# The last block's input projection by 2x2 blocks with seven products, its token-major part and the linear recurrence inside it

## The chip, the cores and the metric

The kernel runs on one core of a Trainium2 chip. A core has TensorE (matmuls), VectorE, ScalarE, GpSimd and SyncE, each with an instruction queue of its own; they meet only at semaphores. The metric is the device time of one execution in microseconds (us). SBUF is the core's on-chip memory of 128 partitions, PSUM the memory into which TensorE accumulates.

## What is computed

Two models in a row on one sequence of 2048 tokens of width 1024: two blocks of a diffusion-style mixer, then one block of linear recurrences. All is fp32. The change is in the input projection of the last block and in two of its users:

```
def second_block(x, c, norm_w, w_ada, b_ada, w_in, ...):
    h = rmsnorm(x, norm_w) * (1 + scale) + shift
    p = h @ w_in                      # 2048 x 1024 by 1024 x N_IN
    # a_x 512, a_g 512, hg_q 512, hg_f 512, hg_i 512, hg_g 512, z 1024, xbc 1536, dt 16
    a = causal_conv(a_x, 4 taps); xbc = silu(causal_conv(xbc, 4 taps))
    y_lru = rg_lru(a, ...) * silu(a_g)
    # hg_f gives a log decay and its running sums; hg_i is wanted token-major
def rg_lru(x, wa, ba, wx, bx, lam):
    r = sigmoid(x @ wa + ba); i = sigmoid(x @ wx + bx)      # blocks of 64 x 64
    log_a = -8 * r * softplus(-lam); a = exp(log_a)
    b = sqrt(-expm1(2 * log_a)) * (i * x)
    h_t = a_t * h_(t-1) + b_t
```

## The kernel before

The program is a row of stages, each a block of five instruction lists (one per engine) with its own semaphores and an all-engine barrier at its end (`Stage`, L83). `program` (L2765) calls them. In the last block: `project` ("in_2", tensors `in_...` in the trace), `tokens_lru` ("hi_2", `hi_...`), `mixers` (`mix_...`), `project_out` (`out_...`).

**Matmuls in three parts.** An fp32 operand is split into a head (rounded to fp32r by ScalarE's copy) and a rest (operand minus head, by GpSimd or VectorE). A product is head x head + rest x head + head x rest (`PARTS`, L288), three matmuls in place of one. `h` holds heads and rests of the 1024 x 2048 columns, 8 tiles of 128 rows, for the whole of both stages.

**`project`** (L291). There are 41 tiles of 128 outputs: 4 `conv`, 12 `conv_silu`, 4 `decay`, 20 with Silu, 1 copy. Each takes 4 chunks of 512 columns x 3 parts x 8 rows of tiles = 96 matmuls (L450; the first two tiles at L436). TensorE runs tile behind tile; two PSUM halves of 2048 columns alternate, as do two weight buffers. ScalarE makes a tile's head (L463), GpSimd its rest (L615), and each tile is emptied by ScalarE (L505, L513, L489). For convolution tiles VectorE does 4 instructions of 2048 columns (L546, L549); for decay tiles ScalarE does Sigmoid, Abs, Exp, Ln and VectorE four steps that read PSUM (L556 to L564), and only then is the PSUM half free. GpSimd issues the stores.

**`tokens_lru`** (L1835). Of `w_hi` 512 columns, in 16 tiles of 128 tokens x 24 matmuls (L1909), with the recurrence in eight units of 128 channels x 1024 tokens between: gates on TensorE (L1898), Sigmoid, Tanh, Exp, Square, Sqrt on ScalarE (L1942 to L1955), products and the scan on VectorE (L1997 to L2009). It reads back `ax` and `gates`, which `project` stored.

The order is written by hand in each engine's list; no scheduler stands behind it. In the rows below `SPq` and `POOLq` are DMA issues on SyncE's and GpSimd's queues.

## Time and profile before

| | us |
|---|---|
| median of 3 runs (4538.61 to 4540.83) | 4540.7 |
| the profiled execution's own time | 4536.25 |
| its span in the profile | 4534.6 |
| TensorE busy | 3932.5 (87%) |
| VectorE, ScalarE, GpSimd busy | 2488.9, 1576.4, 1070.6 |
| `project` "in_2", first load to last matmul | 2550.9 to 3477.9 |
| seam to `tokens_lru`, until its matmuls run on | 3477.9 to 3518.1 |
| `tokens_lru` to its last matmul; to the mixers' first load | 3630.1; 3642.9 |

The profile is one execution. Its views used here: busy time by stretch (each engine's busy us and instruction count, the granted clock of TensorE as a share of 2.4 GHz, the DMA engines' busy share and GB/s), the chain of work that ended last, the timeline of an engine, and the durations of one line. Ends of matmuls are modelled and they are pipelined: a 128x512 matmul shows about 0.39 us though one ends every 0.23; a few records are missing, so durations of groups are used, not counts.

### The profile page before, as it was taken

To read this page: it belongs to the slowest core of one execution; us is meant where nothing else is said; L and a number is where in the kernel's file an instruction comes from. 1 tells how busy PE (TensorE), PEld (TensorE's weight loads), DVE (VectorE), ACT (ScalarE), POOL (GpSimd) and SP (SyncE) were. 2 spreads that over 40 slices of the span, in tenths; PEclk is the share of its full clock that TensorE was granted. 3 is DMA by queue.
4 is the path that set the end of the run, shared out by engine and by line. 5 is a ranking of instruction groups with operands and counts; after the bars stand their busy time and mean duration, and the time that the engine had idled before them with its cause. 6 is when DMAs were issued, how large, how long until landed. Compare 5 with 4: busy or idle time off the path is not lost. (4 is left out here: it accounts for less than half of the span.)

```text
span 4534.6 us, 51807 instructions
## 1 busy us (share of the span) xinstructions
PE 3932.5 (87%) x19448; PEld 3243.2 (72%) x19448; DVE 2488.9 (55%) x3379; ACT 1576.4 (35%) x2589; POOL 1070.6 (24%) x879
## 2 busy tenths in 40 slices
PE   4659998798796999879889799999997968886998
PEld 2548886687575888768657588878885757775886
DVE  2645943687375594378736643330000479995564
ACT  3331102676222110267522212231111755554331
POOL 1421110121111111012111111111110046664454
PEclk7779999899997999989999899999998989998999
DMA  6341122422474112232245421131111356554453
GB/s 236 106 164 56 70 79 88 100 64 83 142 248 142 59 70 79 89 100 66 83 154 205 170 84 70 70 144 70 77 75 65 127 153 151 148 140 162 177 193 114
DMA packets 315762, 529.50 MB, mean 117 GB/s; under 512 B 26790, under 2 KB 203686, under 8 KB 299592
## 3 DMA queue, kind: packets, MB, share of 16 engines
q1 hardware_dynamic: 277002, 353.97, 25.0%
q0 software_dynamic: 38544, 172.69, 10.2%
q8 instruction: 131, 2.15, 0.2%
q14 instruction: 85, 0.70, 0.1%
HBM read 373.57 MB, written 153.00 MB: 116 GB/s over the span
## 5 line engine op out<-in xcount | busy, mean ns | idle before, releaser
L450 PE MATMUL in_ps<-h,in_wp 128*128 128x512 f32 x6624 | 1508.4, 390 | 10.0 <-POOL in_wp L615 10.0
L450 PEld LDWEIGHTS in_ps<-h,in_wp 128*128 128x128 f32 x6624 | 1247.2, 188 | 270.9 <-POOL in_wp L615 11.6
L1714 PE MATMUL out_ps<-out_y,out_wp 128*128 128x512 f32 x2976 | 689.2, 393 | 33.1 <-ACT out_y L1569 25.9
L1714 PEld LDWEIGHTS out_ps<-out_y,out_wp 128*128 128x128 f32 x2976 | 562.0, 189 | 159.7 <-issue 31.8
L585 DVE SCALAR_TENSOR_TENSOR cy<-cu,in_cw,cy 128x2048 f32<-128x2048 f32 x120 | 314.5, 2621 | 4.3
L898 PE MATMUL att_O<-att_pT,att_vs 128*128 128x512 f32 x960 | 302.1, 423 | 0.0
L513 ACT ACTIVATE in_ob<-in_ps 128x2048 f32<-128x2048 f32 x37 | 69.7, 1884 | 664.0 <-PE in_ps L450 664.0
L1631 POOL TENSOR_TENSOR out_wp<-out_w,out_wp 128x2048 fp32r<-128x2048 f32 (+1 forms) x48 | 192.5, 4010 | 412.6 <-ACT out_wp L1562 412.4
L615 POOL TENSOR_TENSOR in_wp<-in_w,in_wp 128x1024 fp32r<-128x1024 f32 x75 | 201.4, 2687 | 284.4 <-ACT in_wp L463 249.7
L1022 DVE TENSOR_TENSOR att_pT<-att_T,att_pT 128x512 fp32r<-128x512 f32 x320 | 219.5, 686 | 73.4 <-ACT att_pT L951 65.1
L1977 DVE TENSOR_SCALAR hi_z<-hi_z 128x4 f32<-128x4 f32 x1 | 0.2, 172 | 463.6 <-ACT hi_z L1934 463.6
L1001 DVE CUSTOM_DVE_ANT_0 att_S<-att_S,att_mk,att_nsink 128x640 f32<-128x640 f32 x256 | 227.0, 887 | 8.0 <-PE att_S L878 7.7
L951 ACT ACTIVATE att_pT<-att_T 128x512 fp32r<-128x512 f32 x320 | 190.3, 595 | 89.0 <-PE att_T L886 88.8
L940 ACT ACTIVATE att_prob<-att_S,att_nm 128x640 f32<-128x640 f32 x256 | 203.7, 796 | 49.6 <-DVE att_nm L1001 44.7
L463 ACT ACTIVATE in_wp<-in_w 128x1024 fp32r<-128x1024 f32 x75 | 79.3, 1057 | 371.2 <-ACTq L481 226.1
L436 PE MATMUL in_ps<-h,in_wp 128*128 128x512 f32 x576 | 144.0, 414 | 63.9 <-ACT h L470 63.9
L886 PE MATMUL att_T<-att_ident,att_prob 128*128 128x128 f32 x1280 | 193.4, 274 | 0.0
L436 PEld LDWEIGHTS in_ps<-h,in_wp 128*128 128x128 f32 x576 | 113.4, 198 | 94.5 <-ACT in_wp L463 65.1
L832 POOL TENSOR_TENSOR att_qs<-att_qf,att_qs 64x512 fp32r<-64x512 f32 x64 | 82.2, 1285 | 384.6 <-ACT att_qs L933 384.6
L629 POOL DMA_DIRECT2D gates<-in_ob x36 | 20.6, 573 | 630.2 <-ACTq L516 630.2
L898 PEld LDWEIGHTS att_O<-att_pT,att_vs 128*128 128x128 f32 x960 | 157.2, 190 | 14.9 <-DVE att_pT L1022 0.9
L886 PEld LDWEIGHTS att_T<-att_ident,att_prob 128*128 128x128 f32 x1280 | 152.3, 141 | 10.9 <-DVE att_pT L1022 0.4
(485 smaller groups left out, 6209.3 us busy)
## 6 DMA issues: line engine op xcount, KB each, us to landing
in_w<-in_w_in SPq DMA_DIRECT2D x75, 512.0 KB, 3.3
gates<-in_ob POOLq DMA_DIRECT2D x36, 1024.0 KB, 4.2
out_w<-in_w_out SPq DMA_DIRECT2D x32, 1024.0 KB, 4.8
out_mw<-in_w_ada_rows SPq DMA_DIRECT2D x48, 512.0 KB, 3.6
att_qf<-q SPq DMA_DIRECT2D x64, 256.0 KB, 4.3
out_yr<-y SPq DMA_DIRECT2D x16, 1024.0 KB, 7.0
x<-out_x POOLq DMA_DIRECT2D x64, 256.0 KB, 3.8
out_yr<-y SPq DMA_DIRECT2D x32, 512.0 KB, 5.6
```

What stands on the lines that cost most here:

```text
L436: mm = nc.tensor.matmul(ps[:, q, cc], wp[:, q, i, k], h[:, j, k, cc], start=(n + k == 0), stop=(n == 2 and k == KT - 1))
L450: mm = nc.tensor.matmul(ps[:, q, c * W:(c + 1) * W], wp[:, q, i, k], h[:, j, k, c * W:(c + 1) * W], start=(n + k == 0), stop=(n == 2 and k ...
L585: stt(y[:, t], u[:, t, k:k + N], cw31[:, t, k:k + 1], y[:, t], ALU.mult, ALU.add).then_inc(tapped, 1)
L615: pool.tensor_tensor(wp[:, q, 1], wt[:, q], wp[:, q, 0].bitcast(F32), ALU.subtract).then_inc(parted, 1)
L886: tr = nc.tensor.transpose(psT[:, n % 2, j * P:(j + 1) * P], prob[:, b % 2, 2 * j + g, kt * P:(kt + 1) * P], ident[:])
L898: mm = nc.tensor.matmul(psO[:, b % 2], vs[:, at, part, g * HD:g * HD + P], pT[:, r, side], start=(u + n == 0), stop=(u == U - 1 and n == 2))
L940: nc.scalar.activation(prob[:, b % 2, hh], psS[:, n % 2, S0:S0 + NK], ACT.Exp, bias=nm[:, b % 2, hh:hh + 1], scale=-1.0, accum_out=den[:, ...
L951: nc.scalar.activation(pT[:, m % 4, 0], psT[:, n % 2], ACT.Copy).then_inc(led, 1)
L1001: nc.vector.tensor_tensor_reduce(out=S, in0=S, in1=m, scale=1.0, scalar=nsink[:, 1, hh:hh + 1], op0=ALU.add, op1=ALU.min, accum_out=nm[:, ...
L1022: tt(pT[:, m % 4, 1], psT[:, n % 2], pT[:, m % 4, 0].bitcast(F32), ALU.subtract).then_inc(freed, 1)
L1631: pool.tensor_tensor(wp[:, u % NW, 1], wt[:, u % 2], wp[:, u % NW, 0].bitcast(F32), ALU.subtract).then_inc(parted, 1)
L1714: mm = nc.tensor.matmul(ps[:, u % NB, :W], wp[:, u % NW, a, k], y[:, c % 2, b, k], start=(i + k == 0), stop=(i == 2 and k == KY - 1))
```

## The change

`project` and `tokens_lru` are replaced for the last block by one stage, `project_lru`. Its names:

- The sequence is worked in two halves of 1024 columns (p = 0, 1), each of V = 23 units: 22 pairs of output tiles (2 conv, 6 conv_silu, then decay, silu, decay, silu, eight silu, two hi) and one single tile (dt), between.
- A pair is a 2x2 block product: two tiles of outputs x two 512-row halves of the depth, by two chunks of 512 columns. It is done as seven products of 12 matmuls (3 parts x 4) in place of eight. `sums(i)` on VectorE makes the four combined weight blocks; `difference` on GpSimd makes the combined column blocks once per half; `h` holds seven column blocks.
- The products land in three PSUM banks (X, Y, Z) of a double buffer. ScalarE copies product 0 to `p1` (`first_product`) and empties X (`empty`); VectorE adds (`second`, `fourth` twice, `upper`, `lower`), each reading one PSUM bank.
- Each product has its own head (ScalarE) and rest (GpSimd), in a ring `wp` of four, three ahead.
- hi tiles come out channel-major and are turned on TensorE by 128x128 transposes (`turn`), copied by `move`, stored token-major.
- The recurrence's units run inside units 12 to 20 of each half, one per two units: gates on TensorE, the rest between the heads and additions. `decay` and the recurrence share buffers.
- SyncE issues all loads and stores; tiles leave through a ring `ob` of three slots. The weight layout is changed on the host in order only.

```diff
+    RING, AHEAD, NOB = 4, 3, 3
+    BANK = (X, Y, Z, Y, X, Y, Z)
+            def weights(i):
+                wait(sp, parted, base(i - 1) if i >= 2 else 0)
...
+                sp.dma_start(raw[:, i % 2, 0:n], w_d[t:t + n].rearrange("a p k n -> p a k n")).then_inc(w_in[i % 2], 16)
...
+                if i + 2 < NU:
+                    weights(i + 2)
+                if i >= 1:
+                    store(i - 1)
...
+            def difference(p, n):
+                for k in range(KH):
+                    if n == 2:
+                        pool.wait_ge(shifted, p * KT + KH + k + 1)
+                        tt(column(2, k), column(5, k), column(2, k), ALU.subtract).then_inc(differed, 1)
+                    elif n == 1:
+                        pool.wait_ge(hparted, p * 28 + k + 1)
+                        pool.wait_ge(differed, p * 16 + k + 1)
+                        tt(column(1, k), column(2, k), column(0, k), ALU.add).then_inc(differed, 1)
...
+            def product(i, n):
+                g = base(i) + n
+                if n == 0:
+                    wait(pe, emptied, i - 1)
+                elif n == 1 and i >= 2:
+                    pe.wait_ge(combined, combos(i - 1))
+                elif n == 3:
+                    pe.wait_ge(combined, combos(i) + 1)
+                elif n == 4:
+                    pe.wait_ge(copied, i + 1)
+                elif n >= 5:
+                    pe.wait_ge(combined, combos(i) + n - 3)
+                times(i, n, n, BANK[n], n < 3, g).then_inc(prod, 1)
...
+            def silus(i):
+                act.wait_ge(combined, combos(i + 1))
+                empty(i, ACT.Silu)
...
+            def fourth(i):
+                dve.wait_ge(prod, base(i) + 4)
+                tt(u4[:], p1[:], ps[:, i % 2, Y], add).then_inc(combined, 1)
+                dve.wait_ge(combined, combos(i) + 2)
+                if kind(i) in ("silu", "hi"):
+                    free(dve, i, 1)
+                tt(target(i, 1, 1), u4[:], ps[:, i % 2, Z], add).then_inc(combined, 1)
...
+            for i in range(NU + 1):
...
+                if i and pair(i - 1):
+                    lower(i - 1)
...
+                if convs:
+                    convolve(i - 1, 0)
...
+                if kind(i - 2) == "decay":
+                    decay(i - 2, 1)
...
+                second(i)
+                if convs:
+                    convolve(i - 1, 1)
+                if lru_of(i, 1) is not None:
+                    widen(lru_of(i, 1))
...
+                fourth(i)
+                if i + 1 < NU:
+                    sums(i + 1)
+                if kind(i - 1) == "decay":
+                    decay(i - 1, 0)
+                if lru_of(i, 1) is not None:
+                    double(lru_of(i, 1))
...
+                upper(i)
...
+                if lru_of(i, 1) is not None:
+                    scan(lru_of(i, 1))
...
-        with nc.sbuf_tensor("h_2", [P, 2, KT, SEQ], F32R) as h:
-            project(nc, "in_2", h, SEQ, t["w_in_2"], [("conv", 4, ax, 1.0), ("conv_silu", 12, xbc, 1.0), ("decay", 4, (hk, hcum, hkc), 1.0),
-                                                      (ACT.Silu, 20, gates, 1.0), (ACT.Copy, 1, dt, 1.0)],
-                    (xT, row12, gain2[:, :, 0], mod2[:, 0:KT, 0]), taps4=(t["taps_2"], t["tap_bias_2"]))
-            tokens_lru(nc, "hi_2", h, SEQ, t["w_hi_2"], HW, hi, ax, t["lru_wa_2"], t["lru_ba_2"], t["lru_wx_2"], t["lru_bx_2"],
-                       t["lru_lambda_2"], gates[0:4], y[0:4])
+        project_lru(nc, "in_2", t["w_in_2"], (xT, row12, gain2[:, :, 0], mod2[:, 0:KT, 0]), (t["taps_2"], t["tap_bias_2"]),
+                    (ax, xbc, hk, hcum, hkc, gates, dt, hi),
+                    (t["lru_wa_2"], t["lru_ba_2"], t["lru_wx_2"], t["lru_bx_2"], t["lru_lambda_2"], y))
```

How it stands in the built program, at three places. VectorE in the convolution tiles, before (after the columns are made):

```order
L528 SCALAR_TENSOR_TENSOR in_ob<-in_ob,gain,in_reset 128x512 x8
L531 SCALAR_TENSOR_TENSOR h<-in_ob,mod,h 128x512 x8
L534 MEMSET in_ub 128x2x3
L546 TENSOR_SCALAR in_ob<-in_ub,in_cw,in_cb 128x2048
L549 SCALAR_TENSOR_TENSOR in_ob<-in_ub,in_cw,in_ob 128x2048 x3
```

VectorE in a convolution unit now, from `second` to `lower` (L2413 `second`, L2449 to L2454 `convolve`, L2417 and L2421 `fourth`, L2403 to L2408 `sums`, L2428 `upper`, L2432 `lower`):

```order
L2413 TENSOR_TENSOR in_u<-in_p,in_ps 128x512
L2449 TENSOR_SCALAR in_ob<-in_ov,in_cw,in_cb 128x1024
L2452 SCALAR_TENSOR_TENSOR in_ob<-in_ov,in_cw,in_ob 128x1024 x3
L2454 COPY in_tails<-in_ov 128x3
L2417 TENSOR_TENSOR in_u<-in_p,in_ps 128x512
L2421 TENSOR_TENSOR in_ov<-in_u,in_ps 128x512
L2403 TENSOR_TENSOR in_S<-in_w 128x512
L2405 TENSOR_TENSOR in_S<-in_S,in_w 128x512
L2406 TENSOR_TENSOR in_w<-in_w 128x512
L2408 TENSOR_TENSOR in_S<-in_w,in_S 128x512
L2428 TENSOR_TENSOR in_ov<-in_p,in_ps 128x512
L2432 TENSOR_TENSOR in_ov<-in_u,in_ps 128x512
```

Between the convolutions of two tiles there now stand additions on whose end TensorE's products wait.

VectorE around the decay tiles, before:

```order
L566 MEMSET in_reset 128x2048
L568 MEMSET in_reset 128x16
L556 SCALAR_TENSOR_TENSOR in_ub<-in_ps,in_ub 128x2048
L560 TENSOR_TENSOR in_kb<-in_ub,in_ps 128x2048
L562 SCALAR_TENSOR_TENSOR in_ub<-in_reset,in_ub 128x2048
L564 TENSOR_TENSOR in_kb<-in_ub,in_kb 128x2048
```

and now, from the end of `fourth` of the unit behind a decay unit to `second` of the next:

```order
L2408 TENSOR_TENSOR in_S<-in_w,in_S 128x512
L2460 SCALAR_TENSOR_TENSOR in_ov<-in_ov 128x1024
L2463 TENSOR_TENSOR in_ov<-in_ov 128x1024
L2465 SCALAR_TENSOR_TENSOR in_ov<-in_ov 128x1024
L2467 TENSOR_TENSOR in_ov<-in_ov 128x1024
L2428 TENSOR_TENSOR in_ob<-in_p,in_ps 128x512
L2432 TENSOR_TENSOR in_ob<-in_u,in_ps 128x512
L2460 SCALAR_TENSOR_TENSOR in_ov<-in_ov 128x1024
L2463 TENSOR_TENSOR in_ov<-in_ov 128x1024
L2465 SCALAR_TENSOR_TENSOR in_ov<-in_ov 128x1024
L2467 TENSOR_TENSOR in_ov<-in_ov 128x1024
L2413 TENSOR_TENSOR in_u<-in_p,in_ps 128x512
```

The four steps of a decay tile stand once before `upper` and `lower`, and once more before `second`.

ScalarE in the recurrence, before (one unit):

```order
L1942 ACTIVATE hi_R<-hi_G,hi_par 128x1024
L1943 ACTIVATE hi_I<-hi_G,hi_par 128x1024
L1947 ACTIVATE hi_T<-hi_R,hi_dec 128x1024
L1948 ACT_TABLE_LOAD
L1948 ACTIVATE hi_R<-hi_R,hi_dec 128x1024
L1951 ACTIVATE hi_A<-hi_R 128x1024
L1925 ACTIVATE hi_ob<-hi_ps 128x512
L1955 ACT_TABLE_LOAD
L1955 ACTIVATE hi_T<-hi_T 128x1024
```

and now, from the root of a recurrence unit to the copy of the next unit's first product:

```order
L2292 ACT_TABLE_LOAD
L2292 ACTIVATE in_ov<-in_ov 128x1024
L2198 ACTIVATE in_wp<-in_w 128x512
L2198 ACTIVATE in_wp<-in_S 128x512
L2232 ACT_TABLE_LOAD
L2232 ACTIVATE in_ob<-in_ps 128x512
L2240 ACTIVATE in_ob<-in_ob 128x512
L2242 ACTIVATE in_ob<-in_ob 128x1024
L2218 COPY in_p<-in_ps 128x512
```

The Silus of the unit before (L2232 to L2242) now stand between the root and the copy that `second` reads.

## Rows read from the trace of the kernel before

**Rows 1.** Busy time by stretch, over both stages; columns as told above.
```profile
2550.90:2565.60 14.70, 0.02 (x1) 0.05 (x1) 5.55 (x9) 2.89 (x4) 1.98 (x1) 0.50 0.97 362
2565.60:2613.30 47.70, 47.70 (x192) 37.86 (x193) 41.82 (x59) 23.05 (x33) 5.65 (x3) 0.92 0.37 135
2613.30:2934.70 321.40, 321.40 (x1419) 266.23 (x1418) 134.49 (x65) 68.33 (x44) 45.15 (x31) 1.00 0.20 76
2934.70:3050.20 115.50, 106.22 (x443) 86.83 (x442) 45.18 (x16) 52.50 (x34) 19.04 (x19) 0.94 0.38 141
3050.20:3477.90 427.70, 427.32 (x1886) 353.61 (x1884) 0.00 (x0) 55.21 (x38) 53.89 (x37) 1.00 0.17 68
3477.90:3518.10 40.20, 9.99 (x14) 4.05 (x14) 8.04 (x32) 7.38 (x11) 1.59 (x3) 0.58 0.35 118
3518.10:3630.10 112.00, 111.94 (x434) 82.65 (x434) 56.57 (x48) 90.19 (x88) 10.60 (x20) 0.98 0.36 125
3630.10:3642.90 12.80, 0.00 (x0) 0.00 (x0) 3.72 (x3) 0.60 (x1) 1.07 (x2) 0.67 0.42 143
```
**Rows 2.** The chain that ended last, in `project_out`: start, us, what.
```profile
4261.71 87.09 PE out_ps L1714 x384
```
**Rows 3.** TensorE's timeline (start, us, line) behind a decay wait; that stretch's clock.
```profile
2966.31 46.58 PE L450 MATMUL in_ps<-h,in_wp 128*128 128x512 f32 x192 [4.69 <-POOL in_wp L615]
...
2965.00:2970.00 5.00, 3.69 (x9) 2.92 (x10) 0.00 (x0) 4.97 (x4) 1.26 (x1) 0.54 1.05 410
```
**Rows 4.** TensorE's timeline: gates of one recurrence unit, then tokens.
```profile
3529.64 1.88 PE L1898 MATMUL hi_G<-hi_A,hi_wa 128*128 128x512 f32 x4
...
3532.67 11.46 PE L1909 MATMUL hi_ps<-hi_wp,h 128*128 128x512 f32 x48
```
**Rows 5.** TensorE's timeline in the mixers: 128x128 transposes.
```profile
3713.88 0.27 PE L2629 MATMUL mix_psM<-mix_ident,mix_B 128*128 128x128 f32 x1
3713.99 0.60 PE L2632 MATMUL mix_psX<-mix_ident,mix_x 128*128 128x128 f32 x4
```
**Rows 6.** Timeline of SyncE's queue and VectorE at the start; DMA rate there.
```profile
2551.23 0.43 SPq L397 DMA_DIRECT2D in_ub<-x  x1
...
2558.42 0.75 DVE L528 SCALAR_TENSOR_TENSOR in_ub<-in_ub,gain,in_reset 128x512 f32<-128x512 f32 x1 [14.41 <-DMA in_ub<-x]
...
2555.00:2557.00 2.00, 0.00 (x0) 0.00 (x0) 0.00 (x0) 0.00 (x0) 0.00 (x0) 0.50 1.04 403
```
**Rows 7.** Durations of single lines: ns least/median/most, first and last start, form.
```profile
L2001 DVE TENSOR_TENSOR hi_T<-hi_T,hi_I x8: 1224/1225/1226, 3529.2 to 3628.8; 128x1024 f32<-128x1024 f32 x8
...
L2215 POOL TENSOR_TENSOR mix_X<-mix_X,mix_q x16: 1264/1272/1281, 3659.5 to 4082.9; 128x512 f32<-128x512 f32 x16
...
L546 DVE TENSOR_SCALAR in_ob<-in_ub,in_cw,in_cb x16: 1346/1347/1740, 2611.1 to 2920.2; 128x2048 f32<-128x2048 f32 x16
...
L2502 DVE TENSOR_TENSOR mix_state<-mix_state,mix_dec x32: 678/1158/1165, 3694.1 to 4121.9; 128x512 f32<-128x512 f32 x32
...
L2505 DVE TENSOR_TENSOR mix_state<-mix_state,mix_psX x32: 686/687/689, 3694.8 to 4123.0; 128x512 f32<-128x512 f32 x32
...
L2005 DVE TENSOR_TENSOR_SCAN hi_A<-hi_R,hi_T x8: 2290/2291/2291, 3530.4 to 3630.3; 128x1024 f32<-128x1024 f32 x8
...
L1925 ACT ACTIVATE hi_ob<-hi_ps x16: 580/584/598, 3539.9 to 3631.4; 128x512 f32<-128x512 f32 x16
```
**Rows 8.** DMA issues in `project`: KB each, median us from issue to landing.
```profile
gates<-in_ob POOLq DMA_DIRECT2D x20, 1024.0 KB, 4.2
in_w<-in_w_in SPq DMA_DIRECT2D x19, 512.0 KB, 3.3
```
**Rows 9.** Busy time by stretch: VectorE's small operations on the rates.
```profile
3500.00:3505.00 5.00, 5.00 (x8) 1.90 (x7) 3.72 (x23) 1.40 (x4) 0.00 (x0) 0.53 0.00 0
```
**Rows 10.** ScalarE's timeline in a decay tile: a table load and what follows.
```profile
2943.57 1.28 ACT L494 ACT_TABLE_LOAD   x1
2944.87 1.92 ACT L494 ACTIVATE in_ub<-in_ub 128x2048 f32<-128x2048 f32 x1
```

More of the change, by code:

```diff
@@ new lines, in _ @@
+            for g in range(AHEAD):
+                rest(g)
+            difference(0, 2)
+            difference(0, 1)
+            for i in range(NU):
+                p, v = divmod(i, V)
+                last = v == V - 1 and p == 0
+                if last:
+                    difference(1, 2)
+                for n in range(7 if pair(i) else 2):
+                    rest(base(i) + n + AHEAD)
+                    if v == 0 and n == 0:
+                        difference(p, 3)
+                        difference(p, 6)
+                    if last and n == 2:
+                        difference(1, 1)
@@ L1919, in _ @@
+            for i in range(NU):
+                if not pair(i):
+                    single(i)
+                    continue
+                for n in range(7):
+                    if kind(i - 1) == "hi" and n in (1, 3):
+                        turn(i - 1, n // 2)
+                    if lru_of(i, 0) is not None and n in (4, 6):
+                        gates(lru_of(i, 0), (n - 4) // 2)
+                    product(i, n)
+            for a in range(2):
+                turn(NU - 1, a)
         @block.scalar
@@ L1993, in _ @@
[L1993 to L2009 removed]
+                dve.wait_ge(chain, count[0])
```

687 lines of the change are left out of this document (546 added, 141 removed).

## The prediction

> **What bounds the kernel now.** I read the granted clock and busy time by stretch first, then TensorE's order in time, then the durations line by line. The last block's projection and its token-major stage take 1092.0 of the 4534.6 us [rows 1]. In its bulk TensorE is never idle: 321.4 us busy of 321.4, 427.3 of 427.7. So there the number of matmuls is the time; 384 of them take 87.09 us [rows 2], 0.2268 us each. The rest of the stage is gaps: 14.7 us until the first matmul; 4.2 us too many in the first 192 (47.7 against 43.5); two waits of 4.6 to 4.7 us in the decay tiles; 40.2 us at the seam to the token-major stage; 12.8 us at the end. After the decay wait the granted clock was 0.54, mostly the 1.2 GHz level, and 192 matmuls took 46.58 us in place of 43.5 [rows 3]: such a wait costs 3.0 us more than itself.
>
> **Matmuls removed.** Before 4320 (41 tiles x 96, 16 tokens x 24); now 22 pairs x 84 x 2 halves + 2 x 48 = 3792. At 0.2268 us that is 860.0 us. The eight gate groups stay: a group of four fp32 matmuls takes 3.03 us (3529.64 to 3532.67) [rows 4], 24.2 us. New are 64 transposes, (0.60 - 0.27)/3 = 0.11 us each by the nearest rows [rows 5], 7 us (bounds 3 and 10). The floor of TensorE is 891 us. A pair's unit needs 19.05 us, a product 2.72. If start and end were as short as before, the stage would take about 925.
>
> **Start and end.** Before, the first columns came as 1 MB behind 1 MB of row: 7.2 us from issue to use [rows 6]. Now 1 MB of weights, 0.5 MB of row and 2 MB of columns stand ahead; at 403 GB/s [rows 6] plus latency, 11.7 us. Scaling (1.23 us per 128x1024 row [rows 7]), shifts, heads, rests and GpSimd's 16 differences of 1.27 us [rows 7] then feed seven products in a chain; `difference(0, 1)` waits for `difference(0, 2)`, and `difference(p, 3)` and `(p, 6)` follow. Walked from the first columns at 11.7 us: scaling of four rows to 16.6, the second 2 MB scaled by 22, shifted by 24; the first rests behind them at 25; `difference(0, 2)` to 27, `difference(0, 1)` to 33, where product 1 can run; then `difference(0, 3)` to 40, with `second` behind its rests on VectorE and product 3 at 41 to 44; `difference(0, 6)` to 46, its rests at 47.5, `fourth` behind them at 48, products 5 and 6 to 54. So unit 0 ends 54 us after the stage begins, of which 19 is matmul: 35 us idle (bounds 28 and 45: each of the steps without lock, or one rest more in each) against 18.9 before. The end (`lower`, two `turn`s, copies, two stores, barrier) I put at 15 us, between 12 and 20, against 12.8. The seam's 40.2 us goes, 3.0 + 1.4 us of work in it apart.
>
> **Convolution units (16).** VectorE had 1 + 3 ops per tile; now, per unit of 19.05 us, it has two tiles of 0.7 + 3 x 1.25 (128x1024), four `sums`, five additions that read PSUM of 0.69: 15.6 us. GpSimd has seven rests of 1.27: 8.9. These two collide. A VectorE addition with both inputs in SBUF took 1158 ns in the middle and 678 at the least, one with an input in PSUM 686 to 689 always [rows 7], on the same stretches with GpSimd busy. The Trainium skill (SBUF — State Buffer, "Who interferes with whom") says that a VectorE instruction with two SBUF inputs and a GpSimd one that reads SBUF exclude each other for the whole instruction; the rows agree. With 12.1 us of VectorE's 15.6 of that form and about 1.1 us lost per rest, less the quarter that falls beside PSUM additions, a unit takes 15.6 + 5.7 = 21.3 us. `second` and `fourth` gate products 3 and 5, so TensorE follows: +2.1 us x 16 = 34 us. Bounds: 0 (all hidden) and 15.6 + 8.9 = 24.5, 87 us.
>
> **A new wait in every silu unit.** `fourth` writes into the store ring `ob`, whose slot must be free of tile (i-1, 0). SyncE issues that store only behind `weights(i+2)`, which waits for the last rest of unit i: after product 2 (8.2) + head + rest, 10.2 us into the unit. 1 MB of loads and 0.5 MB of store then need about 6 us (3.3 us for 512 KB, 4.2 for 1 MB [rows 8]). So `fourth` ends at 16.9 in place of 12.3. Product 6 waits for it from 16.3: 0.6 us. But `sums`, and all that VectorE has behind them, is 4.6 us later.
>
> **Decay units (4 pairs of units).** Behind `sums` stands `decay(i, 0)`: 3 x 1.23 + 2.29 [rows 7] and a rest or two, 7.6 us: 20.5 to 28.1; `upper` and `lower` end at 29.5, 10 us into the next unit, where `decay(i, 1)` (7.6) stands ahead of `second`: it ends 18 us in; product 3 was due at 8.2. TensorE waits 9.7 us, + 3.0 of clock, + 0.6: 13.3 us, times four 53. Taken away are 9.3 + 6.2 us of the old decay tiles. `rates()` (23 small ops take 3.7 us busy of 5 [rows 9]) adds 1 us. Without the ring wait 5.5 us per pair (22 in all); with full exclusion 18 (72).
>
> **Recurrence units (8 pairs).** In the odd unit the chain `sums`, `double` (22.0), root (23.1), multiply (24.4), scan (2.29 us), carry, a rest (28), `lower` (28.7) ends 9.1 us into the next unit. ScalarE's `silus` wait for `lower`; its table load lies in that wait, and 2.3 us of Silu (0.58 + 0.6 + 1.1 [rows 7]) and the copy of the first product (0.6) follow, `second` at 12.7. Product 3 was due at 8.2: 4.5 us, + 0.3 for the reload of A, + 3.0 of clock. Six such: 47. The two before the single tile wait from 5.4 to 12.0, 9.6 with the clock: 19. The odd units add 0.65 x 8 = 5. Sum 71 us (bounds 15, if the ring is free in time, and 100).
>
> **Middle transition.** Units 21 to 23 carry 8 scalings, 16 differences, 28 heads and rests and four `turn`s beside their own work. Walked: `turn(21, 0)`, due at 2.7 us of unit 22, waits for `lower(21)` behind four scalings, 3.6 us; `turn(21, 1)` for `move`, 2.2; the rest of product 6 stands on GpSimd behind `difference(1, 1)`, 3.2; in unit 23 `second` and `fourth` stand behind the rests of `difference(1, 3)` and `(1, 6)`, 6.6 us; with some clock 20 us (8 if GpSimd is never late, 35 if each wait also costs the clock).
>
> **What is hidden.** The stores move from GpSimd's queue to SyncE's, and the projection's weights are read twice: some 24 MB more over 1100 us, 21 GB/s beside the 68 to 141 of the old stages [rows 1], where 403 has been seen [rows 6]; TensorE waits for them only through the order of SyncE's queue above. ScalarE has seven heads of 0.6, two copies and two Silu in a convolution unit, 8 us of 19 (0.58 us per 128x512 [rows 7]), and is no bound there. If it were late, `copied` would hold `second`; apart from the recurrence that cover is wide.
>
> The rule that speaks most against the schedule's table switches is also a page's. In the rows a load takes 1.28 us and the next activation starts 0.02 us behind it [rows 10]. The Trainium skill (ScalarE: Activation LUTs, "What ACT_TABLE_LOAD costs") adds a drain of some 1.4 us to each switch; the rows show none. If it came, two switches on the recurrence's path would cost about 2.8 us more per pair, 22 in all.
>
> **Sum.** 891 + 35 + 34 + 53 + 1 + 71 + 20 + 15 = 1120 us against 1092.0: +28. The profiled execution's own time was 4536.25, the median 4540.7 is 4.5 above it. On the median that is 4540.7 + 28: **4568 us**, rounded down.
>
> **Rivals.**
> - *TensorE stays the bound* (0.33). The ring slot is free before `fourth` wants it, or the lock is mild. Speaks for it: 925 us of near-floor, and every order has slack of three products in the weight ring. Then decay costs 22, recurrence 15 to 20, convolution 17 to 34, transition 15: 891 + 35 + 25 + 22 + 18 + 15 + 15 = 1021, 71 us faster, 4470; from there to 4525. It decides from a store that lands before 12 us into the unit.
> - *Full exclusion* (0.12). VectorE waits out every rest: 87 us for convolution in place of 34, 72 for decay in place of 53, 90 for recurrence in place of 71: +28 + 91, 4660 at the far end, 4600 to 4660 by how much of it comes.
> - *A drain at each table switch* (0.03), by bounds from rows: as the forecast with 22 more, 4590. The page's rule above; the rows of the load [rows 10] speak against it.
> - *Gains and stalls cancel* (0.08): 4541: the forecast with 28 us of its 124 in decay and recurrence not there.
> The forecast, 4545 to 4600, has 0.44. That the change doesn't drop matmuls is excluded by the order of the built kernel.
>
> **The numbers.** A measurement here can tell about 0.2%, 9 us. Faster: 0.33, the first rival. Within: 0.08 and 0.02 of the forecast's lower edge, 0.10. Slower: 0.42 + 0.12 + 0.03 = 0.57. The range leaves out the far half of the first rival and the far part of the second: 4488 to 4628. For the slower cases alone, 4550 to 4625.
>
> **What would show it.** In the changed profile: the stage from the first `in_ov` load to the mixers' first load at about 1120 us; matmuls of 128x512 in it 3792 less lost records; convolution units spaced 21.3 us apart; `sums` and convolution lines of VectorE with means above their minima, PSUM additions at 0.69; VectorE idle before L2421 some 4 us each in silu units, released by a DMA of a store; TensorE idle in two waits of about 10 us per half at decay, of about 4.5 us every second recurrence unit, released by L2413; granted clock near 0.9 in them and 1.0 in the convolution units. Wrong if L2421 waits for nothing, if the convolution units come at 19 us, or if the recurrence pairs take 41 us.

## The result

The changed kernel takes 4694.18 us (median of 4 runs, 4688.82 to 4707.13), the kernel before 4539.65 beside it (4538.05 to 4540.83): ratio 1.0345, 95% interval 1.0323 to 1.0366. It is 3.4% slower. The direction was predicted, the size was not: 4568 was forecast, and 4694 lies outside the range of 4488 to 4628.

The stage, from the first load of weights (2552.72) to the mixers' first load (3795.04), takes 1242.3 us, against 1092.0 before and 1120 forecast. What follows it is as long as before, so the loss of 150 us and the miss of 122 us both lie in this stage. The same view as [rows 1], now for the changed kernel: start, the end of unit 0, seven convolution units, the first half's recurrence, the passage to the second half, convolution units of the second half, its recurrence, the end. Columns are length, busy time of TensorE, its weight loads, VectorE, ScalarE and GpSimd, granted clock, DMA share, GB/s.

```profile
2552.70:2571.30 18.60, 0.00 (x0) 0.00 (x0) 9.70 (x9) 7.04 (x9) 4.50 (x5) 0.50 0.96 363
2571.30:2623.10 51.80, 30.06 (x85) 20.74 (x86) 42.03 (x40) 24.59 (x42) 39.38 (x23) 0.70 0.07 23
2625.90:2780.80 154.90, 137.49 (x589) 109.26 (x588) 139.04 (x134) 47.92 (x74) 81.34 (x49) 1.00 0.28 95
2952.00:3186.00 234.00, 183.36 (x716) 140.09 (x715) 95.28 (x99) 109.14 (x148) 96.73 (x63) 0.91 0.36 119
3186.00:3265.00 79.00, 63.62 (x256) 50.59 (x256) 72.17 (x69) 28.47 (x51) 43.83 (x29) 0.89 0.22 68
3272.00:3450.00 178.00, 148.68 (x628) 118.37 (x627) 143.88 (x135) 68.19 (x96) 77.16 (x53) 0.97 0.27 93
3620.00:3780.00 160.00, 133.94 (x526) 103.05 (x527) 54.05 (x61) 66.90 (x93) 55.34 (x40) 0.91 0.29 93
3785.20:3795.00 9.80, 2.21 (x17) 1.70 (x16) 0.69 (x1) 2.15 (x4) 0.00 (x0) 0.91 0.37 108
```

Where [rows 1] had stretches of 321 and 427 us in which TensorE never stood still, no stretch is like that now. In the convolution units it is VectorE that is busy, 139.04 of 154.90 us; in the recurrence nobody is: TensorE 183 of 234, VectorE 95, ScalarE 109. There everyone waits for someone. The list of waits over the stage (engine, line, waited for, us in total, times, longest) names whom:

```profile
ACT in_wp L2198 <- DVE in_S L2405: 258.0, 40, 11.5
DVE in_ob L2421 <- DMA gates<-in_ob: 114.0, 17, 8.5
PE in_ps L2121 <- DVE in_ob L2421: 62.8, 13, 6.4
PE in_ps L2121 <- DVE in_u L2413: 62.3, 28, 7.4
DVE in_ob L2421 <- DMA hk<-in_ob: 36.9, 4, 10.0
PE in_G L2156 <- ACT in_ov L2277: 36.4, 8, 6.3
DVE in_ob L2421 <- DMA hi<-in_ob: 10.4, 1, 10.4
```

`fourth` (L2421) waits 161 us for stores to free its slot of the ring, in 22 of 24 units that write into it. The forecast had the wait, at some 4 us each, and let TensorE lose 0.6 us by it. It loses 62.8 directly, and 36.4 more at L2156, where it waits for the sigmoids of the gates: a wait that the prediction didn't have at all. One even unit of the recurrence shows how the second follows from the first (timeline; lines of matmuls in between left out):

```profile
2957.74 0.63 ACT L2198 ACTIVATE in_wp<-in_w 128x512 fp32r<-128x512 f32 x1 [2.39 <-PE in_ps L2121]
...
2958.19 0.38 SPq L1974 DMA_DIRECT2D in_w<-in_w_in  x1
...
2958.62 0.94 SPq L2000 DMA_DIRECT2D gates<-in_ob  x2
...
2965.67 0.69 DVE L2421 TENSOR_TENSOR in_ob<-in_u,in_ps 128x512 f32<-128x512 f32 x1 [7.31 <-DMA gates<-in_ob]
...
2967.77 0.63 ACT L2198 ACTIVATE in_wp<-in_S 128x512 fp32r<-128x512 f32 x1 [9.41 <-DVE in_S L2405]
...
2968.42 1.28 ACT L2276 ACT_TABLE_LOAD   x1
...
2970.30 0.68 ACT L2277 ACTIVATE in_ov<-in_G,in_par 128x512 f32<-128x512 f32 x1
...
2971.12 3.38 PE L2156 MATMUL in_G<-in_ov 128*128 128x512 f32 x4 [6.28 <-ACT in_ov L2277]
```

SyncE issues 1 MB of weights at 2958.19 and the unit's two stores of 512 KB behind it; the slot is free 7.5 us after the weights' issue. Until then `fourth` stands; behind it on VectorE stand `sums` (L2403 to L2408); for the sum S ScalarE waits 9.41 us with the head of the weights (L2198); and behind that head on ScalarE stand the gates' sigmoids, which have nothing to do with S and could have run from 2959.4, when the gates' matmuls ended. TensorE wants the PSUM bank that they read, and waits 6.28 us. Then the group of four gate matmuls takes 3.38 us in place of the 1.88 of [rows 4]: after the wait of 6.28 us the granted clock is 0.57 (2971.10 to 2974.50), mostly its 1.2 GHz level. The forecast priced the first of these four links only.

The odd unit behind it shows the ring wait reaching TensorE directly. Its products begin at 2977.30, when the last product of the unit before has ended and `lower` (L2432) starts:

```profile
2977.30 0.69 DVE L2432 TENSOR_TENSOR in_ob<-in_u,in_ps 128x512 f32<-128x512 f32 x1 [7.80 <-PE in_ps L2121]
...
2988.69 1.30 POOL L2069 TENSOR_TENSOR in_wp<-in_w,in_wp 128x512 fp32r<-128x512 f32 x1
...
2990.01 0.38 SPq L1974 DMA_DIRECT2D in_w<-in_w_in  x1
...
2997.54 0.69 DVE L2421 TENSOR_TENSOR in_ob<-in_u,in_ps 128x512 f32<-128x512 f32 x1 [8.37 <-DMA gates<-in_ob]
...
2998.28 12.58 PE L2121 MATMUL in_ps<-in_h,in_wp 128*128 128x512 f32 x48 [4.39 <-DVE in_ob L2421]
```

The stores themselves were held back in both units. Here the Silus that they wait for had ended at 2981.53, and they left at 2990.44, 8.9 us later; in the even unit it was 2953.30 and 2958.62, 5.3 us. In between they stood in SyncE's queue behind the issue of the weights, which waits there for GpSimd's last rest of the unit (L2069). Over the stage SyncE waits 707.3 us in 42 times for a rest before it issues weights.

The DMA issues that answer to [rows 8], of the whole program (the first form of each is this stage's):

```profile
in_w<-in_w_in SPq DMA_DIRECT2D x44, 1024.0 KB, 6.1
gates<-in_ob SPq DMA_DIRECT2D x40, 512.0 KB, 7.3
```

And of [rows 7], VectorE's steps of the convolution (ns least, median, most):

```profile
L2452 DVE SCALAR_TENSOR_TENSOR in_ob<-in_ov,in_cw,in_ob x96: 1283/1737/2291, 2625.8 to 3397.7; 128x1024 f32<-128x1024 f32 x96
```

while the additions that read PSUM never left 0.67 to 0.69 us:

```profile
L2421 DVE TENSOR_TENSOR in_ob<-in_u,in_ps x24: 686/687/690, 2821.1 to 3777.9; 128x512 f32<-128x512 f32 x24
```

### The profile page after: what moved, and what is told of

Same layout as the page of the kernel before. It is cut to its first block and busy times, and to the rows that moved or that the text cites. A ratio compares the mean times of both kernels' runs of the same rounds, so it can differ in the third digit from the quotient of the medians.

```text
span 4687.2 us, 52388 instructions
## 1 busy us (share of the span) xinstructions
PE 3895.8 (83%) x18984; PEld 3180.0 (68%) x18984; DVE 2925.8 (62%) x3891; ACT 1798.5 (38%) x3065; POOL 1459.5 (31%) x1111
## 5 line engine op out<-in xcount | busy, mean ns | idle before, releaser
L2121 PE MATMUL in_ps<-in_h,in_wp 128*128 128x512 f32 x3792 | 948.5, 410 | 210.7 <-DVE in_ob L2421 62.8
L2121 PEld LDWEIGHTS in_ps<-in_h,in_wp 128*128 128x128 f32 x3792 | 744.0, 198 | 412.9 <-DVE in_u L2413 77.6
L450 PE MATMUL in_ps<-h,in_wp 128*128 128x512 f32 x2880 | 653.4, 389 | 0.7 <-POOL in_wp L615 0.7
L450 PEld LDWEIGHTS in_ps<-h,in_wp 128*128 128x128 f32 x2880 | 540.4, 188 | 113.7 <-POOL in_wp L615 1.5
L2069 POOL TENSOR_TENSOR in_wp<-in_w,in_wp 128x512 fp32r<-128x512 f32 x180 | 261.5, 1454 | 330.4 <-ACT in_wp L2198 330.4
L2069 POOL TENSOR_TENSOR in_wp<-in_S,in_wp 128x512 fp32r<-128x512 f32 x132 | 214.0, 1621 | 353.3 <-ACT in_wp L2198 352.4
L2198 ACT ACTIVATE in_wp<-in_S 128x512 fp32r<-128x512 f32 x132 | 83.1, 630 | 411.1 <-DVE in_S L2405 258.0
L2198 ACT ACTIVATE in_wp<-in_w 128x512 fp32r<-128x512 f32 x180 | 113.1, 629 | 154.6 <-PE in_ps L2121 139.7
L615 POOL TENSOR_TENSOR in_wp<-in_w,in_wp 128x1024 fp32r<-128x1024 f32 x34 | 102.8, 3025 | 219.5 <-ACT in_wp L463 203.5
L2452 DVE SCALAR_TENSOR_TENSOR in_ob<-in_ov,in_cw,in_ob 128x1024 f32<-128x1024 f32 x96 | 168.7, 1757 | 3.4
```

The lines of the kernel that those rows point to most:

```text
L450: mm = nc.tensor.matmul(ps[:, q, c * W:(c + 1) * W], wp[:, q, i, k], h[:, j, k, c * W:(c + 1) * W], start=(n + k == 0), stop=(n == 2 and k ...
L2069: tt(wp[:, g % RING, 1], weight(g), wp[:, g % RING, 0].bitcast(F32), ALU.subtract).then_inc(parted, 1)
L2121: mm = nc.tensor.matmul(ps[:, i % 2, bank], wp[:, g % RING, a, k], h[:, n, b, k], start=(first and part + k == 0), stop=(part == 2 and k = ...
L2198: nc.scalar.activation(wp[:, g % RING, 0], weight(g), copy).then_inc(led, 1)
```

## How the experiments are read

ScalarE copies the first product of each unit to SBUF once. The distance between two such copies is called the spacing of the unit here; TensorE needs 19.05 us for a unit. Spacing of the changed kernel: 22.1 us in convolution units of the first half, 22.4 of the second; in the recurrence 30.8 and 27.7 for a pair of units, from these rows of the timeline:

```profile
2953.21 0.57 ACT L2218 COPY in_p<-in_ps 128x512 f32<-128x512 f32 x1
...
2984.00 0.58 ACT L2218 COPY in_p<-in_ps 128x512 f32<-128x512 f32 x1
...
3011.69 0.57 ACT L2218 COPY in_p<-in_ps 128x512 f32<-128x512 f32 x1
```

## Experiment: the ring wait alone

Theory: the order of SyncE's queue (weights ahead of stores) is the largest part of the miss. Rival: the steps lengthened by GpSimd are.

```diff
-                if i + 2 < NU:
-                    weights(i + 2)
                 if i >= 1:
                     store(i - 1)
+                if i + 2 < NU:
+                    weights(i + 2)
```

> SyncE issues the stores of unit i-1 before the weight load of unit i+2; nothing else changes. Theory R (the store ring: in the changed kernel the additions of L2421 waited 161 us for stores queued behind a 1 MB load, and the sums, recurrence and Silus behind them came late): VectorE's waits for stores fall from 161 to under 20 us, the pairs of units with the recurrence from some 59 us to some 50, those with decay from 55.6 to 50, and the time from 4694 to about 4590 (4560 to 4620). Theory L (the port that VectorE and GpSimd share): the convolution units stay at 22.1 us and the time falls by less than 30 us. Theory A (ScalarE's order and table loads): less than 30 us too.

Measured: 4556.32 us (4552.51 to 4564.21), before 4543.80 beside it, ratio 1.0028 (1.0016 to 1.0041). Two lines moved ahead of two others take 138 us away by the medians, more than was expected, and L2421's waits for stores fall from 161 us to 3.2 (in 4 times). Two things change. The larger is when the store is issued: in two neighbouring units of this kernel's timeline the stores leave at 2957.68 and 2981.55, the weights at 2967.08 and 2986.54, so the stores no longer stand behind the weights' wait for a rest, which ends 9.4 and 5.0 us after they have left. The smaller is the transfer: the same bytes go over the same queue, and by the page's DMA issues the store lands in 4.4 us in place of 7.3:

```profile
in_w<-in_w_in SPq DMA_DIRECT2D x44, 1024.0 KB, 6.1
gates<-in_ob SPq DMA_DIRECT2D x40, 512.0 KB, 4.4
```

Where L2421 still waits for a store, the wait is short (timeline of this kernel, an even unit):

```profile
2988.22 0.69 DVE L2421 TENSOR_TENSOR in_ob<-in_u,in_ps 128x512 f32<-128x512 f32 x1 [1.50 <-DMA gates<-in_ob]
```

and its list of waits has 6.0 us of TensorE for the sigmoids, not 36.4:

```profile
PE in_G L2156 <- ACT in_ov L2277: 6.0, 8, 0.8
```

Spacings: recurrence 24.2 + 20.5 for the pair above (58.5 before the edit, 44.7 now), units 9 to 11 at 24.0, 22.3, 23.9 (32.4, 23.2, 32.3). The convolution units stay at 22.1, as they must if nothing in them waits for the ring.

## Experiments: what GpSimd's rests cost

```diff
-                tt(wp[:, g % RING, 1], weight(g), wp[:, g % RING, 0].bitcast(F32), ALU.subtract).then_inc(parted, 1)
+                cc = slice(0, P if g < RING else 8)
+                tt(wp[:, g % RING, 1][:, :, cc], weight(g)[:, :, cc], wp[:, g % RING, 0][:, :, cc].bitcast(F32), ALU.subtract).then_inc(parted, 1)
```

> Left out: the weights' rests are made in full only for the first four products, later ones only in 8 of 128 columns, so GpSimd's instruction is short and the waits stay as they are. Theory L: convolution units go from 22.1 to 19.1 or 19.5 us (16 of them, some 45 us), the transitions gain 10, and in all 4694 falls to about 4630; if the lock is the main cause of the whole loss, to 4560. Theory R: the silu units keep their spacing of 27 to 33 us, since the store behind the load is what they wait for, and the time stays above 4620.

Measured: 4541.77 us (4538.65 to 4550.19), ratio 1.0002 (0.9992 to 1.0012). That is 152 us less than the changed kernel, against some 64 by theory L, whose 4560 for contention as the main cause of the whole loss is nearer, and below the 4620 that theory R gave as a floor. Convolution units are exactly 19.0 apart. Units 9, 11, 12, 14 and 16 keep spacings of 28 to 33 us, as theory R said, and L2421 (here L2422) still waits 121 us for stores (161 before), 80 of them for the gates'. By spacings 45 us went in the convolution units, 58 in the recurrence, 29 in decay and 17 in the transition: narrow rests act on every part, and also let SyncE pass its wait for the rests sooner.

> Both edits: the stores first, and the narrow rests (work left out as there). If ring and port are separate terms the gains add: 4694 - 105 - 65, about 4525. If the sum of both is much smaller than the parts, one of them hides behind the other; if TensorE were the bound after both, about 4450.

Measured (both edits): 4438.30 us (4436.12 to 4440.75), ratio 0.9770 (0.9754 to 0.9786). So the narrow rests are worth 118 us on top of the store order, and the order 103 on top of the rests; the two together take 256 us, 34 less than the sum of each alone. The additive case (4525) is missed by far, the third one (TensorE the bound, about 4450) is nearer, though the stage is still 96 us above TensorE's floor. That doesn't tell whether GpSimd's work slowed VectorE, or GpSimd's own late hand-over slowed TensorE: a narrow rest is also handed over sooner. Two kernels split the two.

The first fills the tile three times in place of the subtraction, late as before but reading nothing:

```diff
+                for m in range(3):
+                    q = 3 * (g - RING) + m
+                    wait(pool, filled, q)
+                    ins = pool.memset(wp[:, g % RING, 1].bitcast(F32), 0.0).then_inc(filled, 1)
+                pool.wait_ge(filled, q + 1)
+                pool.sem_inc(parted, 1)
```

> The store-first kernel with one more edit: after the ring's first fill, GpSimd's rest (a subtraction that reads two operands, 1.45 us mean) is replaced by three fills in a row of the same 128x512 tile, which read nothing and are chained, so that the rest is still handed over late (part 1 of each product is zero: that part of the result is left out). It asks why narrow rests were worth 118 us on top of the store order. Theory A (contention: the two-operand subtraction of GpSimd and VectorE's operations on SBUF lengthen each other): convolutions' steps fall back to the 1226 ns of the one that ran alone, conv units are 19.0 to 19.5 apart as with narrow rests, the whole is near 4440 to 4460. Theory B (the late hand-over of the rest paces TensorE): units stay at 22.1, the whole stays near 4556. If fills also lengthen VectorE's operations, both are seen in the mean of the convolution's steps: 1750 ns again.

Measured: 4445.28 us (4442.66 to 4446.10), ratio 0.9785 (0.9769 to 0.9802). In seven convolution units GpSimd was as busy (83.16 us, 81.34 in the changed kernel) and TensorE never idle (busy time by stretch, columns as above):

```profile
2630.60:2763.60 133.00, 133.00 (x588) 110.19 (x587) 108.69 (x134) 48.52 (x74) 83.16 (x148) 1.00 0.32 111
```

The durations of VectorE's steps and of GpSimd's fills (ns least, median, most):

```profile
L2460 DVE SCALAR_TENSOR_TENSOR in_ob<-in_ov,in_cw,in_ob x96: 1283/1285/1290, 2629.7 to 3245.6; 128x1024 f32<-128x1024 f32 x96
...
L2075 POOL MEMSET in_wp<- x924: 516/527/956, 2613.8 to 3532.1; 128x512 f32 x185
```

None of 96 steps is longer than 1.29 us, where 1.74 was the median. With a hand-over as late as before, the gain is there: it is contention. GpSimd's subtraction lengthens these steps, filling doesn't. The late hand-over and the fills themselves cost together no more than the 7 us that part this kernel from the 4438 of narrow rests. The first tap, which has one input, is another matter: beside fills too it takes more than the 811 ns that it has in the median with narrow rests (1692 in the changed kernel, 807 at the least):

```profile
L2457 DVE TENSOR_SCALAR in_ob<-in_ov,in_cw,in_cb x32: 892/1068/1239, 2628.6 to 3241.8; 128x1024 f32<-128x1024 f32 x32
```

The second hands a narrow rest over at once, and then subtracts 448 elements per partition in a scratch tile:

```diff
+                if g >= RING:
+                    wait(pool, filled, g - RING)
+                    tt(scr[:], ident[:, 0:112].unsqueeze(1).broadcast_to([P, KH, 112]), ..., ALU.subtract).then_inc(filled, 1)
```

> The store-first kernel with narrow rests (8 of 128 columns, handed over at once; the others are left out of the result), and behind each of them GpSimd subtracts 448 elements per partition in a scratch tile that nobody reads, about 1.3 us of two-operand work: GpSimd's hand-over is early, its load on the port is there again. Theory A (contention): conv units go back from 19.0 to 21.5 to 22.1 and the whole to 4530 to 4560. Theory B (late hand-over): 19.0 and 4438.

Measured: 4506.46 us (4500.34 to 4512.17), ratio 0.9925 (0.9909 to 0.9942). The contention is back with an early hand-over (the same durations):

```profile
L2457 DVE SCALAR_TENSOR_TENSOR in_ob<-in_ov,in_cw,in_ob x96: 1283/2047/2053, 2626.9 to 3287.4; 128x1024 f32<-128x1024 f32 x96
...
L2074 POOL TENSOR_TENSOR in_scr<-in_ident x308: 926/935/2982, 2608.3 to 3585.7; 128x448 f32<-128x448 f32 x154
```

Units are 20.4 apart, between 19.0 and 22.1, less than expected: the scratch work takes 0.93 us, not the 1.3 that was assumed, and falls on the three long steps, hardly on the first tap (0.81 us median, 0.91 at most). The Trainium skill (SBUF — State Buffer, "Who interferes with whom") says that a VectorE instruction with two SBUF inputs contends with a GpSimd one that reads SBUF and not with one that only writes, and that `tensor_scalar` and `copy` can contend through a mode that takes both ports. Both kernels agree with the first (2047 ns beside reads, 1285 beside fills), and the first tap's 1068 ns beside fills with the second.

## Experiment: is TensorE the bound?

```diff
                 for part, (a, b) in enumerate(PARTS):
+                    if part == 1 and n > 3:
+                        pe.wait_ge(parted, g + 1)
+                        continue
```

> The store-first kernel with 12 of the 84 matmuls of a unit left out (the rest-times-head part of products four to six; the result lacks it), 2.8 us of TensorE a unit; all waits stay. It asks where TensorE is the bound. Theory A: conv units (TensorE waits 2.7 of 22.1 us for VectorE) stay at 21.5 to 22.1; the odd units of the recurrence (20.5 apart, TensorE nearly full) fall by 1 to 2.8; the whole by 25 to 50 us, to 4505 to 4530. Rival (TensorE is the bound everywhere, its matmuls merely slower): 45 units times 2.8, 125 us less, 4430.

Measured: 4514.04 us (4508.36 to 4516.58), ratio 0.9934 (0.9917 to 0.9950), 42 us less than the store order alone, not the 125 of the rival. The places were not those expected: the odd units of the recurrence stayed at 20.5 to 21.6, so TensorE doesn't bound them, while the convolution units fell, from 22.1 to 21.0 in the mean of the first half (20.3 to 22.4) and from 22.4 to 20.6 in the second. So these units are not bound by VectorE's queue alone. They are a loop through both engines: VectorE's only longer idle time is 2.0 us a unit before `lower`, which waits for the last product of its own unit, and TensorE waits for `second` and `fourth`. Matmuls taken away shorten the loop too.

## Experiments: the two other orders in the recurrence

```diff
+                    if lru_of(i, 0) is not None and n == 5:
+                        gate_sigmoids(lru_of(i, 0), 0)
                     head(base(i) + n + AHEAD)
...
-                    if lru_of(i, 0) is not None and n == 5:
-                        gate_sigmoids(lru_of(i, 0), 0)
```

> The store-first kernel with one more edit: ScalarE's two sigmoids of the gates (first half of the columns) stand ahead of the head of the weights' sum in its queue. All three orders together had been 42 us slower than the store order alone; this tells which of the two others did that. Theory A: it was the order on VectorE (the second sum of products ahead of the gate's product, which frees SyncE, so that loads and stores of the iteration left later), and the sigmoids' order by itself saves the wait of TensorE for them, 0 to 2 us in each of 8 even units: 4540 to 4556. Theory B: the sigmoids' order did it, since the head and with it the rest and the next product come later: 4580 to 4600.

Measured: 4550.08 us (4545.32 to 4560.27), ratio 1.0017 (1.0007 to 1.0027), 6 us less than the store order alone, with intervals that overlap; even units fall by about 1 us each (23.3, 23.9, 23.2 from 24.2, 24.9, 24.0), and the spacings of all units together by 9 us (1031.2 to 1021.9), which shows it more surely than the medians. This order was tried only behind the store order, where TensorE's wait for the sigmoids is 6.0 us in all; what it alone would give where that wait is 36.4 was not run.

The kernel with this and `second` moved ahead of `decay(i - 2, 1)` and `gate` on VectorE:

```diff
+                if pair(i):
+                    second(i)
                 if kind(i - 2) == "decay":
                     decay(i - 2, 1)
...
-                second(i)
```

> Stores first; ScalarE's Sigmoids of the gates before the head that waits for the sums; VectorE's second before the second decay tile and before the gate product of the recurrence. Work and result stay. Theory R plus the order of VectorE: on top of the stores first, the waits for L2413 of about 10 us in four decay pairs and of 4 us in eight recurrence pairs go: another 50 us, to about 4540 (4510 to 4570). If the lock alone were at work it would equal the kernel with the stores first.

Measured: 4597.88 us (4588.75 to 4600.71), ratio 1.0124 (1.0107 to 1.0141). So the two moves on VectorE cost 48 us. The wait that they were to save, TensorE's for L2413, is 40.0 us in all, against 53.7 with the store order alone. Its list of waits and SyncE's code show where the rest comes from:

```profile
DVE in_ob L2421 <- DMA gates<-in_ob: 40.9, 8, 6.3
ACT in_ov L2276 <- PE in_G L2156: 33.5, 6, 7.0
...
PE in_G L2156 <- DMA in_ov<-ax: 24.2, 6, 5.2
```

SyncE opens an iteration with a wait for `scanned`, which `gate` gives. With `gate` behind `second` the wait ends later, and the load of A for the gates, the store and the weights are all queued behind it. The even units are 29 to 31 us again, with some 38 of the 48 us in them. The ring wait has come back by another way. The two moves were not run apart.

## Experiments: the first tap and the tails on ScalarE

The first tap of each convolution becomes an activation on ScalarE (`Identity`, with scale and bias), issued ahead of `head` and behind the copy of the first product; VectorE keeps three taps.

```diff
-                ts(o, ub[:, a, 0:HN], cw[:, n, 0:1], cb[:, n:n + 1], mul, add).then_inc(tapped, 1)
+                nc.scalar.activation(ob[:, tile(i, a) % NOB], ub[:, a, 0:HN], ACT.Identity,
+                                     bias=cb[:, n:n + 1], scale=cw[:, n, 0:1]).then_inc(tap0, 1)
```

> The store-first kernel, and the first tap of each convolution (0.8 to 1.9 us on VectorE, with the copy of the history before it) goes to ScalarE, as one activation with scale and bias. Theory A says that VectorE bounds the conv units (its queue is full, TensorE waits 2.7 us of 22.1 for its additions): with about 2.5 us less on VectorE a unit the spacing falls to 19.8 to 20.5 in the 16 units, the whole to 4515 to 4535, below the 4544 of the kernel before. If ScalarE's extra 1.0 us twice a unit delays the heads instead, units stay at 22 and the whole at 4556.

Measured: 4515.16 us (4511.47 to 4518.21), ratio 0.9937 (0.9921 to 0.9954): faster than before, by 0.6%. Units 20.2 apart in the first half, 19.0 in the second, which doesn't store tails. The copy of three columns (L2463) is the difference:

```profile
L2463 DVE COPY in_tails<-in_ov x16: 1251/1259/1268, 2638.7 to 2787.5; 128x3 f32<-128x3 f32 x16
```

> The kernel with the first tap on ScalarE, and the copy of the last 3 columns (1.26 us on VectorE behind the convolution, though it moves 3 elements a partition) on ScalarE too. With the tap alone, conv units of the first half were 20.2 apart and of the second, which has no such copy, 19.0. If the copy is the difference, the first half falls to 19.0 to 19.3: 8 to 10 us less, 4505 to 4508; if not, 4515.

Measured: 4510.57 us (4505.60 to 4512.56), ratio 0.9928 (0.9911 to 0.9944); units of the first half at 19.0. The whole moved by 5 us, not 8 to 10, within what the medians can tell; the stretch itself moved as expected (7 units by 1.2).

> The same with the gates' sigmoids sooner, as the version that may be fastest. If theory A of the run on the sigmoids' order holds, 4490 to 4507; if B, 4530 to 4550.

Measured: 4499.22 us (4493.72 to 4505.28), ratio 0.9903 (0.9884 to 0.9923), the fastest with the full result: 1.0% under the kernel before, 4.2% under the changed one. Seven convolution units of it, TensorE never idle:

```profile
2628.20:2761.20 133.00, 133.00 (x588) 110.12 (x588) 114.99 (x106) 65.38 (x102) 87.56 (x50) 1.00 0.32 109
```

## Experiment: the start

```diff
+                cc = slice(0, 8 if p == 0 else CH)
...
-                        tt(column(3, k), column(5, k), column(1, k), ALU.subtract).then_inc(differed, 1)
+                        tt(column(3, k)[:, cc], column(5, k)[:, cc], column(1, k)[:, cc], ALU.subtract).then_inc(differed, 1)
```

> The store-first kernel in which GpSimd's 16 differences of the sequence's columns at the stage's start handle 8 of 512 columns (the rest of those sums is left out of the result): it asks whether these, 1.5 to 1.7 us each, are what made the start 16 us longer than predicted. Theory A: heads of columns follow each difference by 1.04 us and TensorE follows the heads, so the first unit gets 12 to 22 us shorter, the whole 4534 to 4545. Rival (the loads and VectorE's scaling set the start): under 5 us, 4551 to 4556.

Measured: 4545.25 us (4541.41 to 4550.90), ratio 1.0007 (0.9998 to 1.0017). The stage is 1091.6 us in place of 1105.2, 13.6 less, and all of the gain lies ahead of unit 1's first copy (58.3 us from the first load, 73.1 with the store order alone). In the changed kernel four differences take 5.9 to 9.2 us where 5.1 was forecast, and the first four wait for the shift, which waits for scaling (timeline of the changed kernel):

```profile
2573.91 9.22 POOL L2077 TENSOR_TENSOR in_ov<-in_ov 128x512 f32<-128x512 f32 x4 [10.29 <-ACT in_ov L2202]
...
2583.09 6.73 POOL L2081 TENSOR_TENSOR in_ov<-in_ov 128x512 f32<-128x512 f32 x4
...
2592.32 5.90 POOL L2084 TENSOR_TENSOR in_ov<-in_ov 128x512 f32<-128x512 f32 x4
...
2598.18 6.78 POOL L2087 TENSOR_TENSOR in_ov<-in_ov 128x512 f32<-128x512 f32 x4
```

28.6 us for 16, of which 20 were in the walk. With them all but gone the start still costs 36 us, as much as was forecast with them in, so other steps of the walk were too short as well; which ones was not taken apart.

## Where the prediction was wrong

Idle time of TensorE over its floor of 891 us, by part of the stage, from the spacings (unit 0 from the first load; units 1 to 7 and 24 to 30; 8 to 11 and 31 to 34; 12 to 20 and 35 to 43; 21 to 23; the end). The transposes' 7 us and roundings keep the columns a few us from the stage's length. The last two kernels are the store order with narrow rests, and the fastest one. The rows go by units, not by cause: of the four waits behind a second decay tile only two lie in units 8 to 11 and 31 to 34 (units 10 and 33), the other two in units 12 and 35, which are counted with the recurrence, while the forecast's 54 has all four.

| part | forecast | changed | store order | + narrow rests | fastest |
|---|---|---|---|---|---|
| start | 35 | 51 | 51 | 48 | 51 |
| 14 convolution units | 30 | 45 | 45 | 0 | 0 |
| decay | 54 | 70 | 36 | 9 | 30 |
| recurrence, single | 71 | 145 | 49 | 20 | 42 |
| transition | 24 | 35 | 29 | 15 | 29 |
| end | 15 | 10 | 10 | 10 | 10 |
| stage, us | 1120 | 1242 | 1105 | 987 | 1047 |

**The step that failed** is the one headed "A new wait in every silu unit", in two of its terms and in what it let follow. It took the landing at 6 us after the weights' issue, and it was 7.5. It took that issue at 10.2 us into the unit; in the odd unit shown above it came 12.7 us into it (2977.30 to 2990.01). The rest for which it waits was late: three rests stood in a row on GpSimd from 2985.20, since two of their heads had waited on ScalarE behind Silus and sigmoids, and the second took 2.29 us. The wait is 7.3 us in the mean (161 in 22 times) and not 4. Worse was what it let follow: "Product 6 waits for it from 16.3: 0.6 us." TensorE waited 62.8 us in 13 times, 4.3 to 6.4 each; the two terms, 2.5 and 1.5 us late, on top of the 0.6 make 4.6 of it, against 4.39 in this unit. To that come 36.4 us in 8 times for sigmoids that stand on ScalarE behind a head that waits for the sums that stand behind `fourth`. The prediction walked VectorE's queue behind the wait, and not the queues of those who wait for VectorE. The 96 us between "changed" and "store order" in the recurrence and 34 in decay are its price by experiment, 138 by the medians.

**Recurrence.** The stall in the even unit behind scan, `lower` and Silu was right in its mechanism, and much too dear. TensorE waits for L2413 62.3 us in 28 times, but only 14.8 of them in the six even units that were meant, 1.5 to 3.4 each and not 4.5 (with the store order 1.1 in the first half, 2.2 in the second). Before the single tile it waits 3.8 and 3.6 us for the copy of the first product (L2218), not 6.6. Another 27.0 are the decay tiles' four. Of the 49 us that the recurrence costs with the store order, 15 lie in units 12 and 35, so 33 stand against the 71 forecast (47 + 19 + 5).

**Decay.** TensorE waits 6.2 to 7.4 us for L2413 in units 10, 12, 33 and 35, and not 9.7. "Without the ring wait 5.5 us per pair (22 in all)" measured 36 in the table's row and 15 more in units 12 and 35, 51 in all; with narrow rests as well, 9 in the row and 10 in those two units.

**Luck.** The forecast, 4568 and a stage of 1120, lies close to the store-order kernel, 4556 and 1105, which has no ring wait to speak of. That confirms nothing: there start and convolution are 31 us above their terms, and recurrence and decay 40 below theirs.

**Convolution.** Forecast 21.3 us, 22.1 measured, for another sum. VectorE's queue takes 15.2 us a unit with narrow rests (106.30 in seven) and 15.5 with fills (108.69), about as forecast (15.6). Contention adds 4.7 to the first (139.04/7 = 19.9), less than 5.7. The forecast counted the first tap among the steps with two inputs in SBUF; it has one, but is lengthened all the same (1.69 us in the median, 0.81 with narrow rests). What was missing is the 2.0 us in which VectorE idles before `lower`, and that the copy of the tails, left out of the sum, can cost 1.25 us.

**Start.** 51 in place of 35. The 16 differences take 1.79 us in the mean where 1.27 was put in, and VectorE's rests of the columns (L2390) 1.52 in the median. 13.6 us go with the differences.

**Rivals.** "TensorE stays the bound", 1021 us, was a description of a kernel that the store order and the rests keep apart: either edit alone gave 4542 to 4556, both 4438. The point from which it was to decide, a store that lands before 12 us into the unit, was not enough: with the store order L2421 waits 3.2 us for stores in the whole stage, and the kernel takes 4556; contention holds the other half. Full exclusion would have made the convolution units 24.5 us, and they are 22.1. No drain shows at a table load: the load starts at 2981.55, 0.02 us behind the Silu before it, takes 1.28 us, and L2276 starts 0.01 us behind it.

```profile
2981.55 1.28 ACT L2276 ACT_TABLE_LOAD   x1
2982.84 0.69 ACT L2276 ACTIVATE in_ov<-in_G,in_par 128x512 f32<-128x512 f32 x1
```

**What was right.** Matmuls dropped (3792 records), PSUM additions at 0.69 always, waits before L2421 released by a store's DMA, granted clock 0.91 in the recurrence and 1.00 in convolution units, and the sign. The recurrence and decay had been given bounds of 15 to 100 and 22 to 72 us; decay's 70 is inside, the recurrence's 145 is not.

What stays open: the even units 14, 16, 18 and their like take 23 to 25.5 us in all store-first kernels with the full result but the one with all orders, and 25.5 beside odd units of 17.4 with narrow rests; what holds the pair at 43 was not taken apart.

## What to carry to other kernels

When a wait is put on a slot that a store must free, look at what stands ahead of that store in the queue of the engine that issues it, and at what that waits for: here a load held ready stores back by 5.3 and 8.9 us in the two units shown because it waited for GpSimd's rests, and by some 3 more because its transfer came first, and the order of the two issues was worth 3% of the kernel. Price a new wait by following every queue that stands behind it to the second and third engine, not only the first; then try the order in which independent work (here the sigmoids) can pass. Serving the engine that should be the bound first can lose if something that frees a DMA queue moves back for it.

## What the runs showed of the hardware

- A 512 KB store issued right behind a 1 MB load on one queue landed in 7.3 us; issued ahead of it (by 5.0 and 9.4 us in the two units looked at) in 4.4. The load took 6.1 both times.
- A copy of three elements per partition on VectorE took 0.16 us in all 16 cases beside fills or narrow rests, and up to 1.25 in the changed kernel beside GpSimd's subtractions (0.16 median): not the size of an operation decides what it loses. In the kernel with the tap on ScalarE it lost that much in all 16 cases (1251 to 1268 ns).
- GpSimd's fills (0.52 us for 128x512) left VectorE's two-input steps alone, 1283 to 1290 ns over 96 of them, and lengthened its one-input tap from 0.81 us (narrow rests) to 1.07 in the median; beside full subtractions the tap took 1.69.
